# Attention layer's second gate projection and first output products, and the recurrent layer's first output products, moved to other stretches

## The reference

```
p      = rmsnorm(x) * (1 + scale) + shift, times w_in
lru:   h = scan forward + scan backward of (a, b);  y = (h * silu(gate)) @ w_out
att:   q, k, v, z = split of p; q and k turned by the rotary tables
       o = softmax(q k^T / 8, with a sink) v, 4 groups of 4 heads, 64 wide
       y = (o * silu(z)) @ w_out
x      = x + gate * rmsnorm(y)
```

## Time and profile before

| | us |
|---|---|
| median of 3 runs (3479.17 to 3483.15) | 3479.84 |
| the profiled execution, its own time | 3479.14 |
| its span in the trace | 3477.4 |
| recurrent phase, from its first transfer to its last | 1466.66 to 1708.06 |
| its output phase, from its first transfer | 1710.48 |
| attention phase, from its first transfer | 1818.46 |
| its output phase, from its first transfer | 2245.29 |
| next phase, from its first transfer | 2353.94 |

### The profile page before, as it was taken

How to read it: one execution, slowest core, us unless ns; L and a number is a source line. 1 busy time by engine, 2 the same in 40 slices (tenths; PEclk the granted TensorE clock), 3 DMA queues, 4 the chain that set the end, 5 groups by cost and what they waited for, 6 DMA issues and landing times. The chain is left out here.

```text
span 3477.4 us, 57294 instructions
## 1 busy us (share of the span) xinstructions
PE 3207.1 (92%) x22569; PEld 2080.8 (60%) x22569; DVE 1745.3 (50%) x3559; ACT 1472.9 (42%) x3018; POOL 627.3 (18%) x520
## 2 busy tenths in 40 slices
PE   5689999999999998899689999697999999999998
PEld 2256777777777763455345665344677676767653
DVE  0146666666666641334431344334666666666631
ACT  1225545545545521255322444322555555555521
POOL 0012322322322400011000000001232323232300
PEclk9699999999999999999899999798999999999999
DMA  9720111211111134012201110102111111111124
GB/s 376 261 55 29 54 45 33 55 44 34 54 44 35 41 101 174 16 55 65 107 19 48 40 34 6 75 24 60 36 41 53 41 44 50 43 51 41 41 97 172
DMA packets 214951, 234.22 MB, mean 67 GB/s; under 512 B 19098, under 2 KB 158820, under 8 KB 214564
## 3 DMA queue, kind: packets, MB, share of 16 engines
q1 hardware_dynamic: 214692, 230.64, 20.5%
HBM read 210.94 MB, written 19.66 MB: 66 GB/s over the span
## 5 line engine op out<-in xcount | busy, mean ns | idle before, releaser
L887 PE MATMUL ps<-hT,W 128*128 128x512 f32 (+1 forms) x2688 | 1011.0, 504 | 0.9 <-ACT arena L1094 0.9
L887 PEld LDWEIGHTS ps<-hT,W 128*128 128x128 f32 x2688 | 469.6, 191 | 205.6 <-issue 167.4
L2150 PE MATMUL ps<-arena 128*128 128x512 f32 x832 | 373.6, 606 | 53.2 <-DMA arena<-in_lru_w_out 24.6
L1306 DVE CAST_PREDICATED arena<-mask,ps 128x384 bf16<-128x384 uint32 x448 | 252.7, 564 | 242.7 <-PE ps L956 180.2
L2150 PEld LDWEIGHTS ps<-arena 128*128 128x128 f32 x832 | 160.3, 195 | 252.4 <-issue 252.4
L1130 ACT CAST arena<-ps 128x384 bf16<-128x384 f32 x384 | 166.6, 479 | 339.0 <-PE ps L943 338.1
L1308 DVE CAST_PREDICATED arena<-mask,ps 128x384 bf16<-128x384 uint32 x448 | 250.3, 559 | 0.0
L1847 PE MATMUL ps<-hT,W 128*128 128x256 f32 (+1 forms) x640 | 227.7, 495 | 6.2 <-DMA W<-in_att_w_in 6.0
L1418 POOL TENSOR_TENSOR arena<-arena 128x768 f32<-128x768 f32 (+1 forms) x32 | 43.6, 1361 | 1015.5 <-ACT arena L1166 1015.5
L465 PE MATMUL ps<-hT,W 128*128 128x512 f32 (+1 forms) x576 | 193.8, 499 | 16.6 <-DVE W L1207 10.9
L1281 DVE SCALAR_TENSOR_TENSOR arena<-arena,vec 128x770 f32<-128x770 f32 (+1 forms) x192 | 189.6, 988 | 6.8
(11 more groups left out here) (272 smaller groups left out, 5864.5 us busy)
## 6 DMA issues: line engine op xcount, KB each, us to landing
arena<-in_ada_w SPq DMA_DIRECT2D x24, 2048.0 KB, 19.6
W<-in_gdn_w_in SPq DMA_DIRECT2D x96, 512.0 KB, 4.0
W<-decay_rows SPq DMA_DIRECT2D x64, 384.0 KB, 5.1
arena<-in_gdn_w_out SPq DMA_DIRECT2D x32, 512.0 KB, 12.4
W<-in_gdn_w_out SPq DMA_DIRECT2D x24, 512.0 KB, 3.5
arena<-gated SPq DMA_DIRECT2D x32, 384.0 KB, 10.1
gated<-arena SPq DMA_DIRECT2D x24, 384.0 KB, 2.3
W<-in_lru_w_in SPq DMA_DIRECT2D x16, 512.0 KB, 3.9
```

Of the source, the lines that this page charges most:

```text
L887: mm = pe.matmul(ps[:, b, 0:t1 - t0], env.W[:, slot, i, :], env.hT[:, i, t0:t1], start=(i == 0), stop=(i == KD - 1))
L1306: dve.copy_predicated(half_cols(Mb[d], s, d), wide(env.m4[:, d, lv]), src_m).then_inc(*inm.up(m, lv, d, "m"))
L2150: return pe.matmul(ps[:, bank(n) + i, :], v.g[:, k, t * P:(t + 1) * P], v.w[:, k, i * 512:(i + 1) * 512], start=(k == first), stop=(k == ( ...
```

## The change

1. Recurrent phase. `out_blocks` gives eight places, from the top of the arena downwards, for w_out and gated of k = 0 to 7. The arena is laid out anew, so that five are free from the start and the others lie over buffers of the even blocks. SP loads k = 0 to 4 after it has stored block 5, k = 5 and w_out of 6 and 7 after it has stored block 6, gated of 6 once that store has landed, and gated of 7 after the last store has landed. After its last gate products PE computes the products of k = 0 to 5 for tiles 0 and 1.
2. Attention phase. Z10 and Z11 of group g move from the stretch before the group's scores to the group's own stretch. In the last stretch they lie in slots 36 to 41. SiLU(z) follows at slots 11, 23, 35 and 41. For groups 0 to 2 DVE only copies the values, and POOL multiplies 2 x 768 columns by SiLU(z) after the group's last tile; in group 3 POOL does so for the first tile alone. Stores, and the loads of z's weights, wait accordingly; the load of z's second block for group g comes after Z11 of g - 1.
3. Attention, output. In slots 42 to 51 PE computes 12 products of tile 0, k = 0 to 5, into banks 6 and 7. Their operands are loaded in the phase: k = 0 to 2 at about slot 35, k = 3 to 5 after group 2's store.
4. Output phases. Attention: first 12 products of tile 1, then k = 6 and 7 of both tiles; gated of 6 and all of 7 are loaded in this phase. Recurrent: only k = 6 and 7 remain for tiles 0 and 1, no load at all. The gains stand after these two k. DeltaNet's output phases keep their order.

```diff
 def lru_phase(env, l):
+        def load_out(k):
+            sp.dma_start(ow(k), w_out[:, k]).then_inc(*out_ld[k].up("w"))
+            sp.wait_ge(st.sem, st.at(k))
+            sp.dma_start(ogated(k), a["scratch"][k]).then_inc(*out_ld[k].up("g"))
...
+            if n == LRU_N - 2:
+                for k in range(5):
+                    load_out(k)
+        sp.dma_start(ow(LRU_N - 3), w_out[:, LRU_N - 3]).then_inc(*out_ld[LRU_N - 3].up("w"))
+        sp.dma_start(ogated(LRU_N - 3), a["scratch"][LRU_N - 3]).then_inc(*out_ld[LRU_N - 3].up("g"))
...
         sp.wait_ge(st.sem, st.at(LRU_N - 1))
+        sp.dma_start(ogated(LRU_N - 1), a["scratch"][LRU_N - 1]).then_inc(*out_ld[LRU_N - 1].up("g"))
...
+        pe.wait_ge(pad.sem, pad.at(LRU_N - 1, 1))
+        pe.wait_ge(sgd.sem, sgd.at(LRU_N - 1, 1))
+        for k in range(LRU_AHEAD):
+            pe.wait_ge(out_ready[k][0].sem, out_ready[k][1])
+            for t in range(2):
+                for i in range(2):
+                    pe.matmul(ps[:, 2 * t + i, :], ogated(k)[:, (CT + t) * P:(CT + t + 1) * P], ow(k)[:, i * 512:(i + 1) * 512],
+                              start=(k == 0), stop=False)
...
+ATT_Z_LAST = 41
+ATT_OUT = {42: 1, 43: 1, 44: 1, 45: 1, 46: 1, 47: 1, 48: 3, 49: 1, 50: 1, 51: 1}
+ATT_AHEAD = 6
 def att_plan():
+    for w in range(AKV + 1):
+        uses = [(w - 1 if use[:2] == "Z1" else w, use) for use in ATT_USES]
+        uses = [(g, use) for g, use in uses if 0 <= g < AKV]
...
+        slots = range(ATT_STEP * (w - 1), ATT_STEP * w) if w < AKV else range(ATT_STEP * (w - 1), ATT_Z_LAST + 1)
...
 def att_phase(env, l):
+                sp.wait_ge(ad.sem, ad.at(g, "Z01"))
+                load_z(g + 1, 0)
+            if g >= 2:
+                store(g - 2)
             if g >= 1:
+                sp.wait_ge(ad.sem, ad.at(g - 1, "Z11"))
+                load_z(g, 1)
+        sp.wait_ge(st.sem, st.at(AKV - 3))
+        for k in range(3):
+            load_out(k)
+        store(AKV - 2)
...
+        for k in range(3, ATT_AHEAD):
+            load_out(k)
+        load_w(ATT_AHEAD)
         sp.wait_ge(og.sem, og.at(NT * AKV - 1))
+        store(AKV - 1)
...
                 for use in plan.get((p, third), []):
                     fill(*use)
+                if third == 0:
+                    forward(given, given + ATT_OUT.get(p, 0))
+                    given += ATT_OUT.get(p, 0)
                 for n, i in turns_at(p, third):
                     turn(n, i)
...
-                act.wait_ge(og.sem, og.at(NT * (g - 1) - 1))
+                act.wait_ge(gm.sem, gm.at(g - 2))
                 act.copy(v.sz[g % 2][:, int(use[1]), lanes(use)], src).then_inc(*aev.up(g, use))
...
-            if (p + 1) % ATT_STEP == 0 and (p + 1) // ATT_STEP < AKV:
-                g = (p + 1) // ATT_STEP
+            if p in (ATT_STEP - 1, 2 * ATT_STEP - 1, 3 * ATT_STEP - 1, ATT_Z_LAST):
+                g = p // ATT_STEP
...
+            if g < AKV - 1 or t == 0:
+                dve.tensor_copy(v.gt[g % 2][:, :, c], ps[:, 5, 0:256].rearrange("p (i n) -> p i n", i=2)).then_inc(*og.up(n))
+                return
...
     def gpsimd(pool):
+        def gate(g):
+            c = slice(0, P if g == AKV - 1 else T)
+            pool.wait_ge(szd.sem, szd.at(g))
+            pool.wait_ge(og.sem, og.at(NT * g + (0 if g == AKV - 1 else NT - 1)))
+            gt = v.gt[g % 2][:, :, c]
+            pool.tensor_tensor(gt, gt, v.sz[g % 2][:, :, c], ALU.mult).then_inc(*gm.up(g))
...
+            if g >= 1:
+                gate(g - 1)
+        gate(AKV - 1)
...
 def out_phase(env, l):
-    ahead = TAIL_K if name == "gdn" else 0
+    ready = env.out_ready if name != "gdn" else None
+    ahead = {"gdn": TAIL_K, "lru": LRU_AHEAD, "att": ATT_AHEAD}[name]
...
+        if name == "att":
+            sp.dma_start(g_at(ATT_AHEAD), a["scratch"][ATT_AHEAD]).then_inc(*env.out_ld[ATT_AHEAD].up("g"))
+            for k in range(ATT_AHEAD + 1, KC):
+                sp.dma_start(w_at(k), w_out[:, k]).then_inc(*env.out_ld[k].up("w"))
+                sp.dma_start(g_at(k), a["scratch"][k]).then_inc(*env.out_ld[k].up("g"))
...
+        if name == "att":
+            for k in range(ahead):
+                for i in range(2):
+                    product(1, i, k)
         for k in range(ahead, KC):
...
             if k - ahead < 4:
                 gain(k - ahead)
+        for n in range(KC - ahead, 4):
+            gain(n)
```

More of the change, by code:

```diff
@@ L1679 @@
 ATT_THIRDS = (5, 3, 3)
+ATT_Z_LAST = 41
+ATT_OUT = {42: 1, 43: 1, 44: 1, 45: 1, 46: 1, 47: 1, 48: 3, 49: 1, 50: 1, 51: 1}
+ATT_AHEAD = 6
 def att_plan():
[L1687 to L1691, removed]
+    plan, done, order = {}, {}, []
+    for w in range(AKV + 1):
+        uses = [(w - 1 if use[:2] == "Z1" else w, use) for use in ATT_USES]
+        uses = [(g, use) for g, use in uses if 0 <= g < AKV]
+        order += uses
+        steps = [(g, use, i, c) for g, use in uses for i, c in enumerate(ATT_COST.get(use, ATT_COST.get(use[-1])))]
+        last = {use: max(i for _, u, i, c in steps if u == use) for g, use in uses}
+        slots = range(ATT_STEP * (w - 1), ATT_STEP * w) if w < AKV else range(ATT_STEP * (w - 1), ATT_Z_LAST + 1)
+        each = sum(step[3] for step in steps) / len(slots)
         spent, goal, at = 0.0, 0.0, 0
-        for p in range(12 * (g - 1), 12 * g):
+        for p in slots:
             for third in range(3):
@@ L1696, in att_plan @@
                 here = []
-                while at < len(steps) and (spent < goal - 1e-6 or (p == 12 * g - 1 and third == 2)):
-                    use, i, c = steps[at]
+                while at < len(steps) and (spent < goal - 1e-6 or (p == slots[-1] and third == 2)):
+                    g, use, i, c = steps[at]
                     here.append((g, use, i, i == last[use]))
@@ L1704, in att_plan @@
         assert at == len(steps)
-    return plan, done
+    return plan, done, order
 def att_phase(env, l):
@@ L1733, in att_phase @@
     on_dve = ("kd1", "kp", "qp0", "qp1")
[L1734 to L1737, removed]
+    before = {key: order[i - 2] if i >= 2 else (-1, order[i][1]) for i, key in enumerate(order)}
     def window(t):
@@ L1913, in values, with forward @@
             mm.then_inc(*pv.up(n))
+        def forward(lo, hi):
+            for at in range(lo, hi):
+                k, i = at // 2, at % 2
+                if at == 0:
+                    pe.wait_ge(aev.sem, aev.at(AKV - 1, "Z11"))
+                pe.wait_ge(out_ready[k][0].sem, out_ready[k][1])
+                pe.matmul(ps[:, 6 + i, :], ogated(k)[:, CT * P:(CT + 1) * P], ow(k)[:, i * 512:(i + 1) * 512], start=(k == 0), stop=False)
+        given = 0
         for p in SLOTS:
@@ L2094, in out_phase @@
     TN = range(len(tiles))
[L2095 removed]
+    ready = env.out_ready if name != "gdn" else None
+    ahead = {"gdn": TAIL_K, "lru": LRU_AHEAD, "att": ATT_AHEAD}[name]
     ks = list(range(ahead, KC)) + list(range(ahead))
[L2097 to L2099 removed]
+    joint = name == "gdn"
+    order = [(s[0], int(s[1])) for s in (TAIL_ORDER if joint else OUT_ORDER) if int(s[1]) < len(tiles) and not (last and s[0] != "Y")]
+    turn = {} if last else TAIL_TURN if joint else OUT_TURN
+    if ready:
+        w_at, g_at = out_blocks(env)
+    else:
+        v = carve(env, [("g", (KC, T)), ("w", (KC, D))])
+        w_at, g_at = (lambda k: v.w[:, k]), (lambda k: v.g[:, k])
     wf = env.W[:].rearrange("p a b c -> p (a b c)")
@@ L2105, in out_phase @@
     per = lambda m: [(n, i) for n in TN for i in range(m)]
-    ld = [seq(f"ld{k}", [("g",), ("w",)], 16) for k in range(KC)]
+    ld = [] if ready else [seq(f"ld{k}", [("g",), ("w",)], 16) for k in range(KC)]
+    there = ready or [(sig, sig.at("w")) for sig in ld]
     dgd = seq("diag", [(n, i) for n in range(4) for i in range(4)])
@@ L2138, in bank, with gain_bank @@
     def bank(n):
-        return 2 * (n % 4)
+        return 2 * ((n + 3) % 4 if name == "att" else n % 4)
+    def gain_bank(n):
+        return bank(2 + n // 2) + n % 2
     def side(n):
```

107 lines of the change are left out of this document (70 added, 37 removed).

## The result

| | before | after |
|---|---|---|
| median, first four runs each, us | 3481.10 (3479.17 to 3483.15) | 3423.21 (3419.10 to 3427.15) |
| ratio, with its 95% interval | | 0.9834 (0.9816 to 0.9851) |
| profiled execution, its span | 3477.4 | 3417.8 |

The kernel is faster by 1.7%, 57.9 us by these medians. Forecast was 3427 in 3417 to 3441. In a later series of five runs of the changed kernel against nine of before the medians were 3424.41 and 3476.84, 52.4 us apart (ratio 0.9845, 0.9831 to 0.9858). Single executions of either kernel spread over 7 to 8 us, and where that comes from is a part of what follows.

The account below looks back on a forecast made before the run. PE, busy for 92% of the span, was taken to bound the kernel. The terms -26.5 - 10.3 + 0 + 1 - 16.4 = -52.2 against 3479.1 us gave 3427, in a range of 3417 to 3441.

Parts of the forecast that it names:

- Recurrent layer, -26.5: Recurrent output phase: tile 2 starts 26.8 us earlier, 20.6 of it from products and 3.9 from start; taken as -26.5.
- rival 4: Recurrent layer: early products do little, as SP's barrier waits for the transfer or blocks come late; -22 to -20, chance 0.06.
- First stretch of attention, -10.3: Attention before its first scores: Z10 and Z11, 3.4 and 6.9 us of PE records, leave; -10.3 us.
- inner stretches, 0: Attention's middle stretches: each loses a Z10 and Z11 and gains those of the group before; PE bounds them, 0.
- Last stretch, +1: Attention's last stretch: +6.6 us of added work at full clock, less 5.3 for clock coming back; about +1.
- The sum at full clock: Attention's last stretch: if all the lost clock comes back, the stretch is 3.9 us shorter.
- I take half: Attention's last stretch: gaps of 2 us remain in slots 43 to 47, so half the clock loss returns, 5.3 us.
- the +6.6: Attention's last stretch: added time at full clock from z's weights, fills, SiLU and the new products, +6.6 us.
- Attention's output phase, -16.4: From attention's last barrier to tile 2: less products, start and slow first records; -16.4 us, between -14.7 and -18.0.
- the slow start: Attention's output phase: first records after the gap took 6.68 us instead of 3.4; half of the 3.3 counted as saved.
- rival 1: The clock comes back whole: attention's last stretch gives -3.9, its output phase -18.0; 3421 us, chance 0.2.
- rival 3: Attention: POOL's products, three of 4.0 us and one of 0.6, hold DVE and PE up; +12.6 or 3440, chance 0.06.

Follow-up runs that it names:

- lru_loads_only: The changed kernel with the recurrent layer's output blocks still loaded early, but all its products kept in the output phase (LRU_AHEAD 6 to 0); 3451.95 us.

## Why the prediction was right

**Recurrent layer, -26.5.** Measured -26.2 on average, and from the last store to tile 2 26.6 in the first pair. The split held as well: 4.3 for start and loads, 21.9 for the products and the clock. The feared wait for the last transfer at the barrier (rival 4) does not exist: PE starts 0.75 us after its issue.

**First stretch of attention, -10.3; inner stretches, 0.** Measured -10.4 and 0.0. PE bounded both, so the moved records' own time was the whole answer.

**Last stretch, +1.** Measured -1.5 by the means of three profiles each, -0.4 with lru_loads_only counted in; the profiled pair alone says -4.8. The sum at full clock, 3.9 us less than 87.4 or 83.5, is what the first and third profile show, 82.6 and 82.9. "I take half" was a guess between two outcomes that both occur. In slots 36 to 41 all of the clock came back; from slot 42 on, where it had been 0.75 to 0.83, nearly all of it in some executions and about a third in others (0.97 and 0.85). The mechanism was right; a mean was named where there are two values. The six terms of the +6.6 were not measured one by one.

**Attention's output phase, -16.4.** Measured -16.1 on average, -17.7 in the first pair. The first records after the barrier run at full speed in two of the changed kernel's three profiles, so all of the slow start came back there and half was counted. But the slow start itself was 3.3 us only in the profile that was read; in the other two of before it was 1.9 and 2.3, which brings the average near the forecast. So that the term is met within 0.3 us is in part luck: two deviations cancel.

**The sum.** -52.2 was forecast. The stretches C to G give -54.2 by their means; the second series of runs gives -52.4, the first -57.9. The first profile is rival 1 (3421): it reads 82.6 in F and 95.0 in G, and its time is 3419.58. Its stretches C to G give -59.3 against the first profile of before, and A, B and H, at -3.3, +1.0 and +2.0, nearly cancel. C and G together are 42.3 us shorter by their means, where the prediction asked for about 43. So the forecast's median was about right, 2.6 to 3.8 us above the measured ones, with chance 0.2 for a case that in fact alternates with it. A slip without consequence: the stretches outside, A and H, are 2590 us long and not 2700.

**POOL (rival 3)** was priced too bluntly. One product is 3.44 us, not 4.0. The question was not how often POOL runs, but whether a DVE operation on SBUF falls into that time; in the last stretch the next one begins 0.7 us later. That E stayed at 272.3 us shows that it cost nothing in the inner stretches either.

## What to carry to other kernels

A border between two phases costs the last store, the barrier, the first load and a slow start of PE, one after the other. Loading early removes only the load (4.3 us here); moving products into the gap saves most (21.9 more). In a stretch that waits in turn for several engines, what added PE work costs depends on its place: it can be free ahead of an instruction that waits anyway. Thirteen products, placed by the gaps that the timeline shows, took 51.2 us in both profiles, where ten in the first order took 53 to 60. One pair of profiles misleads in a stretch with a wavering clock: the first pair showed a gain of 4.8 us there, three of each 1.5 on average, which is less than their spread.

## What the runs showed of the hardware that was not expected

- The granted clock after equal gaps differs between executions of one program: after 2.17 us of waiting a transposition ran in 0.66 us once and in 1.12 another time, and F2 came out at 53.2 and 58.7 us. After a gap of 2.6 us it fell too in one profile (twelve score records in 2.00 us) and not in another (1.36). With the gaps filled it still fell in both profiles, to 0.93 over the stretch.
- An operation of 128 x 4 elements on DVE with two SBUF inputs took 0.16 us alone and up to 3.15 us beside a POOL product of 1536 columns, while DVE's reductions out of PSUM kept 0.42.
- The recurrent phase, from its first transfer to its last store, took 239.2 to 242.4 us in three executions of the changed kernel and 240.9 to 242.6 in three of the kernel before; the cause is not known.
